# Low parts of three activation operands computed by VectorE alone, and the first two weight tiles behind each multiplied high parts first

## The chip, the cores and the metric

The kernel runs on one core of a Trainium2 chip. The metric is the device time of one execution in microseconds (us), lower is better. TensorE does the matrix products, VectorE (DVE in the rows) and ScalarE (ACT) the elementwise work, GpSimd (POOL) some of it, and SyncE (SP) issues the transfers between HBM and SBUF.

## What is computed

The reference runs two transformer-like blocks in fp32 on one sequence of 1024 tokens with 1024 features, one after the other. Cut to what matters here:

```python
def first_block(x, ...):
    x = x + _hgrn2_mixer(_rmsnorm(x, norm_mix), w_in, ..., w_out)
    x = x + _squared_relu_mlp(_rmsnorm(x, norm_mlp), mlp_w1, mlp_w2)   # a = relu(h @ w1); (a * a) @ w2
    return _rmsnorm(x, norm_final)

def gated_merge(h, y_four, y_attn, w_gate, w_fo, w_ao, w_o):
    g_f, g_a = split(sigmoid(h @ w_gate))
    merged = g_f * (y_four @ w_fo) + g_a * (y_attn @ w_ao)
    return merged @ w_o

def second_block(x, ...):
    hx = modulate(rms_norm(x, norm1_g), sh1, sc1)
    ...                                             # Fourier mixing, neighbourhood attention
    x = x + g1 * gated_merge(hx, y_four, y_attn, ...)
    hx2 = modulate(rms_norm(x, norm2_g), sh2, sc2)
    x = x + g2 * sqrelu_mlp(hx2, w_mlp1, w_mlp2)
    return x
```

Both MLPs have 4096 hidden features.

## The kernel before

Activations lie feature-major in SBUF: 8 slices (index k) of 128 features by 1024 tokens. A product with a 1024x1024 weight is made in 8 output tiles (index m) of 128 features, each held in one of four PSUM buffers of 128x1024 and accumulated over the 8 slices k. To keep fp32 accuracy with the faster fp32r format, every operand is split in two: a high part (the value rounded to fp32r) and a low part (the value less its high part). A product is then three: high weight by high activation, low weight by high activation, high weight by low activation. A 128x512 matmul is issued for each half of the tokens, so one tile of 8 slices takes 32 matmuls with high activations (L415 and L418) and 16 with low ones (L431, or L425 in a tile that is finished by halves).

The class `Operand` names an activation operand: its high part, its low part, the slices that are made in halves, and `lo_on`, which says for each slice whether DVE ("v") or POOL ("p") subtracts. `on_dve` gives all eight to DVE, `even_pool` and `odd_pool` give every second slice to POOL. Three operands matter here:

- HM is the normalised input of the first MLP, HN that of the second. `normed` (L1573, DVE) multiplies each slice by gain and 1/rms into `HT`; `norm_hi` (L1123, or L1125 with a shift, ACT) rounds it into `Hh`; `norm_lo` subtracts into `Hl` (L1583 or L1585 on DVE, L2035 on POOL). `HT` and `Hl` are the same memory. For HN the shift of the modulation is added too: ACT does it in the rounding, DVE in the subtraction, and for the slices of POOL a further ACT instruction adds it to `HT` first (L1129).
- HG is the merged, gated value. In front of it stands the merging loop over m: ACT makes the two sigmoids (L1526), DVE multiplies the Fourier branch by its gate (L1987), multiplies tile m of the attention output product ("ao", weights w_ao) by the other (L1991), and adds (L1993). Then ACT rounds (L1529) and DVE and POOL subtract (L1996, L2096). The attention output's own operand, `yah` and `yal`, lies in the memory of `Hh`, so the rounding into `Hh` can start only when the last "ao" tile is complete.

Weights come in the order of the list `WT`. SP loads weight n into `Wraw` (2 buffers), ACT makes `Whi` (L1094), DVE makes `Wlo` (L1555), both in rings of 4 buffers. `feed(to)` does this up to a weight number; `upto(name)` allows for four weights ahead of the named one. Weight n needs the buffer of weight n-4, and so waits in the engine's queue until the last product with weight n-4 is complete. Each engine runs its own program in the order in which it is written, and they meet at semaphores.

On TensorE, `fm(name, operand)` makes one output tile: for each k the matmuls with high activations, then all with low ones:

```python
for k in range(kt):
    ...  # wait for high part of slice k: 2 matmuls with wh, 2 with wl
for k in range(kt):
    pe.wait_ge(opd.lo_at(k))
    for c in HALF:
        i = e.matmul(t[:, c], wh[:, k, ms], opd.lo[:, k, c], start=False, stop=k == kt - 1)
```

`sums` makes the sums over features for a norm, with a matrix of ones (L491, L494), `square` the squares for it, `rstd` the 1/rms (L1114, L1116). `mlp(j, operand)` makes 32 tiles "s1" of the hidden layer and, mixed with them, the second product "s2" (L649, L651, L658). "wo2" is the product with w_o behind HG. `x_load` brings back the residual into `R1` once a merged slice has been split.

Of the kernel before, what the change touches and what calls it, by code (L numbers as in the profile page):

```python
# [6 lines left out]
F = mybir.dt.float32  # L7
# [84 lines left out]
def build(nc, xT, vecs, w_in, w_out, m_w1, m_w2, ctxT, c_d, w_ada, w_in2, gains, biasE, biasM, w_gate, w_fo, w_ao,  # L92
          w_o2, m2_w1, m2_w2, ident_d, masks_d, rope_d, dft_d, cd_d, out):
    with ExitStack() as ctx:
# [241 lines left out]
        HM = Operand(3, Hh, Hl, (0,), even_pool)  # L336
        HC = Operand(4, hch, hcl, (), even_pool)
        H2 = Operand(5, Hh, Hl, (0,), on_dve)
        HG = Operand(6, Hh, Hl, (), odd_pool)
        HN = Operand(7, Hh, Hl, (0,), even_pool)  # L340
# [33 lines left out]
        def tensor_program(pe):  # L374
# [29 lines left out]
            def fm(name, opd, kt=8, w=None, m0=0, halves=False, ring="all"):  # L404
# [23 lines left out]
# [4 lines that stand above are left out]
                    if k == kt - 1:  # L432
                        full(i, b, occ)
                    if k % 2:
                        yield

# [189 lines left out]
            def mlp(j, opd):  # L626
                A_h, A_l = ah[j], al[j]
                for kind, i in MLP:
                    if kind == "s1":
                        run(fm((j, "s1", i), opd))  # L630
                        continue
# [275 lines left out]
            for m in range(8):  # L907
# [171 lines left out]
        def scalar_program(act):  # L1079
# [442 lines left out]
            for m in range(8):  # L1522
                feed(upto(("w_ao", m - m % 2)))
                for buf, name in ((gfb, "gf"), (gab, "ga")):
                    act.wait_ge(S("merge_in", m % 4).at(m))
                    e.activation(buf[m % 4][:], buf[m % 4][:], ACT.Sigmoid).then_inc(*S(name).tick(m))  # L1526
            for k in range(8):
                act.wait_ge(S("merged").at(k), full_at(("ao", 7)))
                e.activation(Hh[:, k, :], R1[:, k, :], ACT.Copy).then_inc(*S("hi", 6).tick((k, 0)))  # L1529
# [5 lines left out]
            norm_hi(HN, HT, mc(24))  # L1535
# [8 lines left out]
        def vector_program(dve):  # L1544
# [438 lines left out]
            for m in range(8):  # L1983
                feed(upto(("w_ao", m - m % 2)))
                name, o = ("ao", m), mr2[m % 2]
                dve.wait_ge(S("gf").at(m), S("merge_in", m % 4).at(m))
                e.tensor_tensor(R1[:, m, :], R1[:, m, :], gfb[m % 4][:], ALU.mult).then_inc(*S("fo_gate").tick(m))  # L1987
                dve.wait_ge(S("ga").at(m), full_at(name), S("o_full").at((1, NP - 1)))
# [5 lines left out]
            for k in range(0, 8, 2):  # L1994
                dve.wait_ge(HG.hi_at(k), S("merged").at(k), full_at(("ao", 7)))
                e.tensor_tensor(Hl[:, k, :], R1[:, k, :], Hh[:, k, :].bitcast(F), ALU.subtract).then_inc(  # L1996
# [20 lines left out]
        def gpsimd_program(pool):  # L2017
# [53 lines left out]
            norm_lo(HM, HT)  # L2071
# [22 lines left out]
            for k in range(1, 8, 2):  # L2094
                pool.wait_ge(HG.hi_at(k), S("merged").at(k), full_at(("ao", 7)))
                e.tensor_tensor(Hl[:, k, :], R1[:, k, :], Hh[:, k, :].bitcast(F), ALU.subtract).then_inc(  # L2096
                    *S("lo", 6, "p").tick(k))
            norm_lo(HN, HT, True)

# [113 lines left out]
```

## Time and profile before

| | |
|---|---|
| time, median of 3 runs | 2884.84 us (2884.38 to 2887.16) |
| time of the profiled execution | 2886.22 us |
| its span | 2884.4 us |
| TensorE busy | 2780.8 us (96%) |
| VectorE busy | 1318.2 us (46%) |
| ScalarE busy | 894.0 us (31%) |
| GpSimd busy | 215.9 us (7%) |

The span runs from the first to the last instruction of the profiled execution. A matmul on TensorE counts as busy from its start to its end, and neighbours overlap, so the granted clock has to be read beside the share: TensorE runs at 1.2 or at 2.4 GHz, and 1.00 in the rows is the upper level.

### The profile page before, as it was taken

To read this page: it belongs to the slowest core of one execution; us is meant where nothing else is said; L and a number is where in the kernel's file an instruction comes from. 1 tells how busy PE (TensorE), PEld (TensorE's weight loads), DVE (VectorE), ACT (ScalarE), POOL (GpSimd) and SP (SyncE) were. 2 spreads that over 40 slices of the span, in tenths; PEclk is the share of its full clock that TensorE was granted. 3 is DMA by queue.
4 is the path that set the end of the run, shared out by engine and by line. 5 is a ranking of instruction groups with operands and counts; after the bars stand their busy time and mean duration, and the time that the engine had idled before them with its cause. 6 is when DMAs were issued, how large, how long until landed. Compare 5 with 4: busy or idle time off the path is not lost.

```text
span 2884.4 us, 40780 instructions
## 1 busy us (share of the span) xinstructions
PE 2780.8 (96%) x17644; PEld 2316.4 (80%) x17644; DVE 1318.2 (46%) x1637; ACT 894.0 (31%) x1308; POOL 215.9 (7%) x165
## 2 busy tenths in 40 slices
PE   7999999989999999998899999999898999999999
PEld 5887887768888888887789778877786888888887
DVE  5444464455444454336524565565635333333332
ACT  5444454432211112125322443344324111221111
POOL 1222122110000000005200000000101000000000
PEclk9999999999999999999899999999999999999999
DMA  3101110313334442112323221111721111111111
GB/s 127 38 27 42 38 38 24 102 52 116 123 103 132 131 127 70 52 60 78 111 85 110 65 77 50 52 66 47 259 59 37 52 44 52 46 49 51 44 51 66
DMA packets 211266, 213.08 MB, mean 74 GB/s; under 512 B 6928, under 2 KB 186640, under 8 KB 211088
## 3 DMA queue, kind: packets, MB, share of 16 engines
q1 hardware_dynamic: 211088, 210.48, 23.0%
q8 instruction: 139, 2.28, 0.3%
q14 instruction: 39, 0.32, 0.0%
HBM read 188.44 MB, written 22.02 MB: 73 GB/s over the span
## 4 chain that ended last, share of the span: by engine, by line
PE 74%; DVE 4%; ACT 3%; issue 1%; POOL 1%; DMA 0%; ACTq 0%; DVEq 0%; POOLq 0%; SPq 0%
PE ps L415 11%; PE ps L431 11%; PE ps L418 11%; PE ps L658 8%; PE ps L651 7%; PE ps L649 7%; PE ps L844 2%; PE ps L845 2%; PE ps L849 2%; PE ps L478 2%; PE ps L474 2%; PE ps L476 2%; DVE HT L1573 1%; PE ps L819 1%; PE ps L798 1%
## 5 line engine op out<-in xcount | busy, mean ns | idle before, releaser
L1555 DVE TENSOR_TENSOR Wlo<-Wraw,Whi 128x1024 fp32r<-128x1024 f32 x216 | 268.0, 1245 | 991.1 <-ACT Whi L1094 991.1
L1094 ACT ACTIVATE Whi<-Wraw 128x1024 fp32r<-128x1024 f32 x228 | 239.7, 1057 | 1295.6 <-PE ps L431 627.6
L415 PE MATMUL ps<-Hh,Whi 128*128 128x512 f32 x1600 | 505.8, 398 | 30.2 <-DVE k L1627 10.3
L418 PE MATMUL ps<-Hh,Wlo 128*128 128x512 f32 x1600 | 500.5, 394 | 0.0
L649 PE MATMUL ps<-ah,Whi 128*128 128x512 f32 x1024 | 398.8, 389 | 1.2 <-ACT ah L1271 1.2
L651 PE MATMUL ps<-ah,Wlo 128*128 128x512 f32 x1024 | 398.4, 389 | 0.0
L431 PE MATMUL ps<-Hl,Whi 128*128 128x512 f32 x1568 | 384.0, 394 | 2.9 <-DVE Hl L1996 2.7
L415 PEld LDWEIGHTS ps<-Hh,Whi 128*128 128x128 f32 x1600 | 301.9, 191 | 100.5 <-issue 13.0
L418 PEld LDWEIGHTS ps<-Hh,Wlo 128*128 128x128 f32 x1600 | 305.2, 191 | 65.0
L431 PEld LDWEIGHTS ps<-Hl,Whi 128*128 128x128 f32 x1568 | 293.3, 189 | 68.7 <-DVE Hl L1996 3.5
L658 PE MATMUL ps<-al,Whi 128*128 128x512 f32 x1024 | 253.4, 389 | 0.1
L474 PE MATMUL ps<-Whi,Hh 128*128 128x256 f32 x768 | 223.9, 292 | 10.5 <-ACT Hh L1125 10.5
L649 PEld LDWEIGHTS ps<-ah,Whi 128*128 128x128 f32 x1024 | 192.2, 188 | 42.0 <-ACT ah L1271 2.1
L478 PE MATMUL ps<-Whi,Hl 128*128 128x256 f32 x768 | 220.5, 287 | 5.4 <-DVE Hl L1585 5.4
L658 PEld LDWEIGHTS ps<-al,Whi 128*128 128x128 f32 x1024 | 192.0, 188 | 40.8 <-DVE al L1741 1.0
L651 PEld LDWEIGHTS ps<-ah,Wlo 128*128 128x128 f32 x1024 | 192.2, 188 | 39.9
L476 PE MATMUL ps<-Wlo,Hh 128*128 128x256 f32 x768 | 219.3, 285 | 0.0
L474 PEld LDWEIGHTS ps<-Whi,Hh 128*128 128x128 f32 x768 | 149.3, 194 | 12.5 <-issue 11.0
L478 PEld LDWEIGHTS ps<-Whi,Hl 128*128 128x128 f32 x768 | 148.9, 194 | 7.7 <-DVE Hl L1585 7.7
L476 PEld LDWEIGHTS ps<-Wlo,Hh 128*128 128x128 f32 x768 | 149.4, 194 | 0.0
L1594 DVE SCALAR_TENSOR_TENSOR R<-ps,mods,R 128x1024 f32<-128x1024 f32 (+1 forms) x73 | 92.3, 1266 | 69.3 <-PE ps L658 69.3
L844 PE MATMUL ps<-Hh,Whi 128*128 128x512 f32 x256 | 106.8, 417 | 1.6 <-ACT Vx L1481 1.6
(292 smaller groups left out, 3414.1 us busy)
## 6 DMA issues: line engine op xcount, KB each, us to landing
Wraw<-in_m_w SPq DMA_DIRECT2D x128, 512.0 KB, 3.9
n<-in_w_ada SPq DMA_DIRECT2D x64, 512.0 KB, 3.5
Wraw<-in_w_in SPq DMA_DIRECT2D x56, 512.0 KB, 4.0
R<-in_xT SPq DMA_DIRECT2D x16, 512.0 KB, 4.5
Wraw<-in_w_gate SPq DMA_DIRECT2D x16, 512.0 KB, 4.1
gate_scratch<-gr SPq DMA_DIRECT2D x32, 256.0 KB, 2.3
Wraw<-in_w_out SPq DMA_DIRECT2D x8, 512.0 KB, 4.5
xs_scratch<-R SPq DMA_DIRECT2D x8, 512.0 KB, 3.2
```

Source lines behind the costliest of these rows:

```text
L415: e.matmul(t[:, c], wh[:, k, ms], opd.hi[:, k, c], start=k == 0, stop=False)
L418: e.matmul(t[:, c], wl[:, k, ms], opd.hi[:, k, c], start=False, stop=False)
L431: i = e.matmul(t[:, c], wh[:, k, ms], opd.lo[:, k, c], start=False, stop=k == kt - 1)
L474: e.matmul(o, opd.hi[:, k, c], wh[:, k % 4, :], start=k == 0, stop=False)
L476: e.matmul(o, opd.hi[:, k, c], wl[:, k % 4, :], start=False, stop=False)
L478: i = e.matmul(o, opd.lo[:, k, c], wh[:, k % 4, :], start=False, stop=k == 7)
L649: e.matmul(ps[:, cs], wh[:, k, ws], A_h[:, t % 5, cs], start=k == 0, stop=False)
L651: e.matmul(ps[:, cs], wl[:, k, ws], A_h[:, t % 5, cs], start=False, stop=False)
L658: x = e.matmul(ps[:, cs], wh[:, k, ws], A_l[:, t % 5, cs], start=False, stop=k == 3)
L844: e.matmul(t, wh[:, k, :], Hh[:, k, c], start=k == 0, stop=False)
L1094: e.activation(Whi[n % 4][:], Wraw[n % 2][:], ACT.Copy).then_inc(*S("w_hi").tick(n))
L1555: e.tensor_tensor(Wlo[n % 4][:], Wraw[n % 2][:], Whi[n % 4][:].bitcast(F), ALU.subtract).then_inc(*S("w_lo", "v").tick(n))
```

## The change

For HM and HN the low parts of all eight slices are now DVE's (`on_dve`), for HG too; POOL has no part in any of them, and the additional ACT instruction for HN falls away. A new function `two_tiles` makes the first two "s1" tiles of each MLP and the first two "wo2" tiles: all matmuls with high activations of both tiles, then all with low ones. HG's high part goes to the memory of `Hl`, which is free while the "ao" tiles are made, and its low part to that of `Hh`; so the rounding waits for the merged slice (and for the last gate product, which read `Hl`), and only the subtraction waits for the last "ao" tile. In the merging loop `feed` stands behind the sigmoids of an odd m on ACT, and behind the gating of the Fourier branch of an even m on DVE, where it stood at the head of each even m.

```diff
-        HM = Operand(3, Hh, Hl, (0,), even_pool)
+        HM = Operand(3, Hh, Hl, (0,), on_dve)
...
-        HG = Operand(6, Hh, Hl, (), odd_pool)
-        HN = Operand(7, Hh, Hl, (0,), even_pool)
+        HG = Operand(6, Hl, Hh, (), on_dve)
+        HN = Operand(7, Hh, Hl, (0,), on_dve)
...
+            def two_tiles(names, opd):
+
+                both = []
+                for name in names:
+                    both.append((weight(name), take(name)))
+                    WL[WN[name]] = PS[name][0], (PS[name][1], 0)
+                for (n, wh, wl), (b, occ) in both:
+                    empty(b, occ)
+                    pe.wait_ge(S("w_hi").at(n))
+                    for k in range(8):
+                        for hf, c in enumerate(HALF):
+                            pe.wait_ge(opd.hi_at(k, hf))
+                            e.matmul(psum[b][:, c], wh[:, k, :], opd.hi[:, k, c], start=k == 0, stop=False)
+                        pe.wait_ge(lo_of(n))
+                        for c in HALF:
+                            e.matmul(psum[b][:, c], wl[:, k, :], opd.hi[:, k, c], start=False, stop=False)
+                for (n, wh, wl), (b, occ) in both:
+                    for k in range(8):
+                        pe.wait_ge(opd.lo_at(k))
+                        for c in HALF:
+                            i = e.matmul(psum[b][:, c], wh[:, k, :], opd.lo[:, k, c], start=False, stop=k == 7)
+                    full(i, b, occ)
...
                     if kind == "s1":
-                        run(fm((j, "s1", i), opd))
+                        if i == 0:
+                            two_tiles([(j, "s1", 0), (j, "s1", 1)], opd)
+                        elif i > 1:
+                            run(fm((j, "s1", i), opd))
...
-            for m in range(8):
+            two_tiles([("wo2", 0), ("wo2", 1)], HG)
+            for m in range(2, 8):
                 run(fm(("wo2", m), HG, halves=m == 7))
...
             for m in range(8):
-                feed(upto(("w_ao", m - m % 2)))
                 for buf, name in ((gfb, "gf"), (gab, "ga")):
                     act.wait_ge(S("merge_in", m % 4).at(m))
                     e.activation(buf[m % 4][:], buf[m % 4][:], ACT.Sigmoid).then_inc(*S(name).tick(m))
+                if m % 2:
+                    feed(upto(("w_ao", m - 1)))
             for k in range(8):
-                act.wait_ge(S("merged").at(k), full_at(("ao", 7)))
-                e.activation(Hh[:, k, :], R1[:, k, :], ACT.Copy).then_inc(*S("hi", 6).tick((k, 0)))
+                act.wait_ge(S("merged").at(k))
+                if k == 0:
+                    act.wait_ge(S("g_full").at((1, NP - 1)))
+                e.activation(HG.hi[:, k, :], R1[:, k, :], ACT.Copy).then_inc(*S("hi", 6).tick((k, 0)))
...
-            norm_hi(HN, HT, mc(24))
+            norm_hi(HN, HT, mc(24), on_vector=True)
...
             for m in range(8):
-                feed(upto(("w_ao", m - m % 2)))
                 name, o = ("ao", m), mr2[m % 2]
                 dve.wait_ge(S("gf").at(m), S("merge_in", m % 4).at(m))
                 e.tensor_tensor(R1[:, m, :], R1[:, m, :], gfb[m % 4][:], ALU.mult).then_inc(*S("fo_gate").tick(m))
+                if m % 2 == 0 and m:
+                    feed(upto(("w_ao", m - 2)))
...
-            for k in range(0, 8, 2):
+            feed(upto(("w_ao", 6)))
+            for k in range(8):
                 dve.wait_ge(HG.hi_at(k), S("merged").at(k), full_at(("ao", 7)))
-                e.tensor_tensor(Hl[:, k, :], R1[:, k, :], Hh[:, k, :].bitcast(F), ALU.subtract).then_inc(
+                e.tensor_tensor(HG.lo[:, k, :], R1[:, k, :], HG.hi[:, k, :].bitcast(F), ALU.subtract).then_inc(
                     *S("lo", 6, "v").tick(k))
...
-            norm_lo(HM, HT)
...
-            for k in range(1, 8, 2):
-                pool.wait_ge(HG.hi_at(k), S("merged").at(k), full_at(("ao", 7)))
-                e.tensor_tensor(Hl[:, k, :], R1[:, k, :], Hh[:, k, :].bitcast(F), ALU.subtract).then_inc(
-                    *S("lo", 6, "p").tick(k))
-            norm_lo(HN, HT, True)
```

The order on TensorE at the start of the first MLP, before; Whi_55 and Wlo_59 are the weights of tile "s1" 0, Whi_56 and Wlo_60 those of tile 1:

```order
L415 MATMUL ps<-Hh,Whi_55 128x512 x2
L418 MATMUL ps<-Hh,Wlo_59 128x512 x2
L431 MATMUL ps<-Hl,Whi_55 128x512 x16
L415 MATMUL ps<-Hh,Whi_56 128x512 x2
L418 MATMUL ps<-Hh,Wlo_60 128x512 x2
```

The same place in the changed program, at the seam between the two tiles and at the end of them:

```order
L449 MATMUL ps<-Hh,Whi_55 128x512 x2
L452 MATMUL ps<-Hh,Wlo_59 128x512 x2
L449 MATMUL ps<-Hh,Whi_56 128x512 x2
L452 MATMUL ps<-Hh,Wlo_60 128x512 x2
...
L457 MATMUL ps<-Hl,Whi_55 128x512 x16
L457 MATMUL ps<-Hl,Whi_56 128x512 x16
L415 MATMUL ps<-Hh,Whi_57 128x512 x2
```

The 16 matmuls with `Hl` of tile 0 have moved behind the 32 high ones of tile 1. The third tile (Whi_57) follows as it did.

The order on ScalarE at the end of the merging loop and behind it, before; the gf and ga are the sigmoids of m = 4 to 7, Whi_57 and Whi_58 are high parts of "wo2" weights:

```order
L1094 ACTIVATE Whi_57<-Wraw_53 128x1024
L1526 ACTIVATE gf_174<-gf_174 128x1024
L1526 ACTIVATE ga_178<-ga_178 128x1024
L1526 ACTIVATE gf_175<-gf_175 128x1024
L1526 ACTIVATE ga_179<-ga_179 128x1024
L1094 ACTIVATE Whi_58<-Wraw_54 128x1024
L1526 ACTIVATE gf_176<-gf_176 128x1024
L1526 ACTIVATE ga_180<-ga_180 128x1024
L1526 ACTIVATE gf_177<-gf_177 128x1024
L1526 ACTIVATE ga_181<-ga_181 128x1024
L1529 ACTIVATE Hh<-R_49 128x1024 x8
```

The same place in the changed program:

```order
L1552 ACTIVATE gf_175<-gf_175 128x1024
L1552 ACTIVATE ga_179<-ga_179 128x1024
L1121 ACTIVATE Whi_57<-Wraw_53 128x1024
L1552 ACTIVATE gf_176<-gf_176 128x1024
L1552 ACTIVATE ga_180<-ga_180 128x1024
L1552 ACTIVATE gf_177<-gf_177 128x1024
L1552 ACTIVATE ga_181<-ga_181 128x1024
L1121 ACTIVATE Whi_58<-Wraw_54 128x1024
L1559 ACTIVATE Hl<-R_49 128x1024 x8
```

The four last sigmoids now stand ahead of Whi_58, the high part that has to wait for the last "ao" tile; only that one instruction is left between this wait and the eight roundings.

On VectorE at the same place, the changed program has these rows from the merging of m = 7 on:

```order
L2022 TENSOR_TENSOR mr_183<-ga_181,ps 128x1024
L2024 TENSOR_TENSOR R_49<-R_49,mr_183 128x1024
L1585 TENSOR_TENSOR Wlo_62<-Wraw_54,Whi_58 128x1024
L2028 TENSOR_TENSOR Hh<-R_49,Hl 128x1024 x8
```

The low part Wlo_62 stood ahead of the gating of m = 6, and the subtractions are eight here, where they were four with four more on POOL.

## Rows read from the trace of the kernel before

**Rows 1.** The page, busy time of each engine.

```profile
PE 2780.8 (96%) x17644; PEld 2316.4 (80%) x17644; DVE 1318.2 (46%) x1637; ACT 894.0 (31%) x1308; POOL 215.9 (7%) x165
```

**Rows 2.** Busy time by stretch: PE, PEld, DVE, ACT, POOL, TensorE clock, DMA, GB/s.

```profile
615.00:651.00 36.00, 28.70 (x100) 20.39 (x101) 27.77 (x17) 15.85 (x18) 12.79 (x4) 0.86 0.22 74
700.00:750.00 50.00, 50.00 (x222) 41.41 (x221) 22.64 (x27) 7.75 (x8) 0.00 (x0) 1.00 0.41 135
2061.00:2097.00 36.00, 27.28 (x102) 21.29 (x101) 22.70 (x13) 14.81 (x16) 12.40 (x4) 0.86 0.45 147
2167.00:2204.00 37.00, 30.74 (x101) 21.49 (x100) 26.73 (x16) 19.13 (x21) 11.73 (x4) 0.82 0.06 19
```

**Rows 3.** Waits of TensorE: us in total, times, longest us.

```profile
PE ps L415 <- ACT Hh L1123: 7.6, 6, 2.4
```

**Rows 4.** Timeline of DVE and POOL, start of the first MLP: start, us, instruction.

```profile
618.38 4.59 DVE L1573 SCALAR_TENSOR_TENSOR HT<-R,vec,t 128x1024 f32<-128x1024 f32 x2
621.70 2.47 DVE L1573 SCALAR_TENSOR_TENSOR HT<-R,vec,t 128x1024 f32<-128x1024 f32 x2
627.43 3.37 DVE L1573 SCALAR_TENSOR_TENSOR HT<-R,vec,t 128x1024 f32<-128x1024 f32 x1
631.92 6.80 DVE L1583 TENSOR_TENSOR Hl<-HT,Hh 128x1024 fp32r<-128x1024 f32 x4
618.08 2.61 POOL L2035 TENSOR_TENSOR Hl<-HT,Hh 128x1024 fp32r<-128x1024 f32 x1 [77.00 <-ACT Hh L1123]
```

**Rows 5.** Timeline of ACT and PE, the same place.

```profile
630.84 2.26 ACT L1123 ACTIVATE Hh<-HT 128x1024 fp32r<-128x1024 f32 x2 [2.24 <-DVE HT L1573]
617.99 0.59 PE L415 MATMUL ps<-Hh,Whi 128*128 128x512 f32 x1 [0.37 <-ACT Hh L1123]
622.92 0.73 PE L415 MATMUL ps<-Hh,Whi 128*128 128x512 f32 x2 [1.24 <-ACT Hh L1123]
628.65 1.22 PE L415 MATMUL ps<-Hh,Whi 128*128 128x512 f32 x2 [2.14 <-ACT Hh L1123]
```

**Rows 6.** Timeline of DVE: an operand with all subtractions on DVE, POOL idle.

```profile
1377.79 9.64 DVE L1585 SCALAR_TENSOR_TENSOR Hl<-HT,mods,Hh 128x1024 fp32r<-128x1024 f32 x8
```

**Rows 7.** Chain that ended last, pieces of three stretches: start, us, what.

```profile
650.45 0.45 PE ps L415 x2
...
2061.87 1.06 ACT Whi L1094
...
2096.84 0.45 PE ps L415 x2
...
2104.09 3.63 PE ps L431 x16
...
2187.55 0.85 PE ps L418 x2
...
2203.76 0.45 PE ps L415 x2
```

**Rows 8.** Timeline, end of the merging loop and the first "wo2" tiles.

```profile
2066.62 7.67 ACT L1529 ACTIVATE Hh<-R 128x1024 fp32r<-128x1024 f32 x8
2067.81 1.19 PE L415 MATMUL ps<-Hh,Whi 128*128 128x512 f32 x2 [6.03 <-ACT Hh L1529]
2072.21 0.69 PE L418 MATMUL ps<-Hh,Wlo 128*128 128x512 f32 x2
2072.11 11.20 DVE L1996 TENSOR_TENSOR Hl<-R,Hh 128x1024 fp32r<-128x1024 f32 x4
2093.41 1.06 ACT L1094 ACTIVATE Whi<-Wraw 128x1024 fp32r<-128x1024 f32 x1 [17.81 <-DMA Wraw<-in_w_o]
```

**Rows 9.** Timeline, start of the second MLP.

```profile
2169.68 13.36 DVE L1573 SCALAR_TENSOR_TENSOR HT<-R,modA,b 128x512 f32<-128x512 f32 x8 [0.41 <-ACT b L1116]
2179.49 1.15 ACT L1125 ACTIVATE Hh<-HT,mods 128x1024 fp32r<-128x1024 f32 x1 [2.17 <-DVE HT L1573]
2171.25 0.76 PE L415 MATMUL ps<-Hh,Whi 128*128 128x512 f32 x1 [0.37 <-ACT Hh L1125]
2177.38 1.07 PE L415 MATMUL ps<-Hh,Whi 128*128 128x512 f32 x2
```

## The prediction

> **What bounds the kernel now.** I read the page's busy times first: TensorE is busy for 96% of the span and no other engine for half of it [rows 1]. So only two things can shorten the run: TensorE's idle time, 103.6 us in all, and stretches in which its matmuls run at the lower clock. A table of busy time by stretch shows where these lie. Inside an MLP TensorE is busy for 50.00 of 50.00 us at clock 1.00. At the three places that the change touches it is busy for 28.70 of 36, 27.28 of 36 and 30.74 of 37 us, at 0.82 to 0.86 [rows 2]. I call them A (the first MLP's start), B (merging and "wo2") and C (the second MLP's start). The list of waits says what TensorE waits for there: high parts from ScalarE [rows 3]. The timelines then say who is late behind ScalarE.
>
> At A it is DVE. `normed` instructions follow each other after 1.2 us where nothing is in the way (two in 2.47 us), but one that starts while POOL subtracts takes 3.37 us, and the one at 618.38 ends, by the start of its follower, after 3.4 us [rows 4]. The subtractions come behind them, from 631.92. The last high part is therefore ready at 630.84 + 2.26 = 633.1, TensorE waits up to 2.14 us on the way [rows 5], and the third tile starts at 650.45 [rows 7]. At C it is the same with a 13.36 us row of `normed` [rows 9], and the third tile starts at 2203.76 [rows 7].
>
> At B the last "ao" tile is complete at 2061.87, when ACT converts a weight; then come four sigmoids, and the rounding starts at 2066.62 [rows 7, 8]. TensorE idles for 6.03 us. The low parts of DVE are late too: the four end at 2072.11 + 11.20 = 2083.3 [rows 8].
>
> **The change part by part.** Matmuls cost 3.63 us per 16 at the upper clock [rows 7], so 0.227 us each: 0.91 for one slice's four high ones, 7.26 for a tile's 32, 3.63 for its 16 low ones. At the lower level a pair takes 0.85 [rows 7], a slice 1.7.
>
> *A.* Eight subtractions and eight `normed` all run on DVE without POOL. For the subtraction with nothing on POOL there is a row from elsewhere: eight in 9.64 us, 1.2 each [rows 6]. `normed` of k = 2 starts at 618.38 as before; six slices at 1.195 end at 625.6; ACT adds 1.06 (two take 2.26): high part 7 at 626.7. The subtractions end at 625.6 + 9.6 = 635.2. TensorE starts on k = 0 as before, its second half at 617.99, at the lower clock. It was at the upper one by 622.92 [rows 5]. Until then it falls behind the 1.2 us pace of the slices (1.7 each), and catches up at 0.91. Slice 7 is then done at 627.6 (bound by the high part) to 628.1 (if the clock rises as late as 624.5); I take 627.8. Behind it stand 32 high matmuls of tile 1, to 635.1, and 32 low ones, to 642.3. The low parts are all there at 635.2, the first one is wanted at 635.1 and the last 3.2 us after it: they cost nothing, with 3 us to spare. Gain 650.45 - 642.3 = **8.1 us**.
>
> *C.* `normed` of k = 1 follows 0.66 us after 2169.68, seven slices at 1.195 end at 2178.7. ACT needs 1.15 for one, so the last high part is at 2179.9. ACT has lost four instructions of 1.15 us, which only shortens its queue. The lower clock lasted from 2171.25 to the mixed row at 2177.38 [rows 9], longer than at A. So slices 0 to 3 end at 2172.7, 2174.5, 2176.2, 2177.9, and the other four at about 0.93: 2181.6. Then 14.5 us: 2196.1, where the chain has 2203.76 [rows 7]. Subtractions end at 2178.7 + 9.6 = 2188.3, before the first is wanted (2188.9). Gain **7.6 us**, 8.6 if the clock is no brake.
>
> *B.* ACT's weight conversion at 2061.87 still waits for the last "ao" tile; it ends at 2062.9, and the eight roundings follow directly at 0.95 us each (eight in 7.67, the last taking 1.04 [rows 8]): high part 0 at 2063.9, 7 at 2070.6. This holds if the merged slices are there. Slice 7 needs the last tile (2061.87), two DVE instructions of 1.15 to 1.25: 2064.3, ahead of its turn at 2069.6. Its sigmoids wait only for their transfer, which SP issues when slice 3 is merged. TensorE's idle time falls from 6.03 to about 2.0 us. After 1.24 us of idleness at A the next matmuls were at the upper clock, after 2.14 us at the lower [rows 5]. 2.0 is nearest to the second, so I take the lower clock for 4.6 us, as long as here before (2067.81 to the mixed row at 2072.21 [rows 8]). Slices end at 2065.9, 2067.6, 2069.0, then five at 0.91: 2073.5. With 14.5 us more: 2088.0 against 2096.84 [rows 7]. Gain **8.8 us**; 10.7 if the clock stays up, 7.9 if it is down for 6.5 us. The low parts: DVE makes Wlo_62 until 2065.5, then eight subtractions to 2075.1, wanted from 2080.8. What may be late next is the fifth "wo2" weight, whose transfer stands behind the eight residual loads and was converted at 2093.41 [rows 8]. Each load waits for a low part, and the last low part falls from 2083.3 to 2075.1, so these too come 8 us earlier; the weight is wanted two tiles after tile 1, at 2109.8. Nothing is lost.
>
> *Moved feeds and queues.* In the merging loop conversions of "wo2" weights wait for "ao" tiles 1, 3, 5, 7 as before; only what is behind them changes. On SP nothing is moved, but it waits for low parts of weights from DVE that come one gating (1.2 us) later. The weights are wanted 10 us and more after that. In `two_tiles` tile 0 of A ends at 638.7, and its weight buffer is free then; the next to use it is tile "s1" 4, wanted at 642.3 + 21.8 = 664.1. POOL does nothing at these places any more, and nobody waits for it.
>
> *The sum.* 8.1 + 8.8 + 7.6 = 24.5 us. After each place TensorE runs without a gap (50.00 of 50.00 [rows 2]), so a gain is handed on to the end. The profiled execution took 2886.22, so 2861.7; it was 1.4 us over the median, so the median comes to **2860.3**.
>
> **Where a rule speaks against it.** The four DVE instructions that I add at each place are 4 x 1.2 = 4.8 us on an engine that was already full there (27.77 of 36 us [rows 2], and without a gap from 616.5 to 638.7). The Trainium skill, page "Perfetto Trace Analysis", section "Optimizing Scalar/DVE Operations", holds that with DVE saturated it may make sense to move work to ScalarE or even GpSimd, which is what the kernel before did; though it adds that between DVE and GpSimd this might not help, because they share a port. By its first half alone taking the work back would be a loss of DVE time and the sum that of the second rival below, 2871; by its second half 2860. The trace's 3.37 us beside POOL against 1.2 without it [rows 4, 6] agrees with the second.
>
> **The rivals.**
> *DVE's 3.4 us are not POOL's doing*, but come from ACT or TensorE reading the same tiles, and the subtractions suffer likewise. Then `normed` at A ends at 631.9 as before, eight subtractions of 3.4 us end at 659.1, and the second tile at 659.1 + 0.45 + 3.63 = 663.2: 12.7 us later. At C 2183.0 + 27.2 + 4.1 = 2214.3, 10.5 later; at B nothing. Time 2884.8 + 23 = 2908, slower. It decides from 1.8 us a subtraction on (631.9 + 8 x 1.8 + 4.1 = 650.4 at A). For it: the 3.4 us rows lie where ACT and TensorE are busy too. Against it: eight in 9.64 us, while TensorE multiplies the same operand [rows 6]. Chance 0.02.
>
> *The slow `normed` stay slow, the subtractions take 1.2.* At A high part 7 comes at 633.1 as before; its slice at the lower clock ends at 634.8, both tiles at 649.3, gain 1.1. The low parts, at 631.9 + 9.6 = 641.5, are in time. At C `normed` ends at 2169.68 + 13.36 = 2183.0, the high part at 2184.2, its slice at 2185.9, the tiles at 2200.4, gain 3.4. With B's 8.8: 2871.5. For it: a busy ACT or TensorE is beside every slow one. Against it: POOL's subtraction runs from 618.08 to 620.7, and the instruction behind it ends one undisturbed length later. Chance 0.05. This is what the first half of the rule above (the Trainium skill, "Perfetto Trace Analysis") would come to.
>
> *The clock stays down for the whole first tile*, since TensorE is fed in small pieces. Eight slices at 1.7 us from 617.7: 631.3, gain 4.6 at A; 2172.7 + 7 x 1.7 = 2184.6, gain 4.6 at C; 2065.9 + 7 x 1.7 = 2077.8, gain 4.5 at B; sum 13.7, time 2871. For it: at 2187.55, at the end of a run of unbroken slices, pairs still took 0.85 [rows 7]. Against it: fed in smaller pieces, it still rose at 622.92, 2072.21 and 2177.38. Chance 0.08.
>
> *The merged slices, not ScalarE, set B's pace*, because transfers of the gates come late. They run behind SP's waits and keep the DMA queues full in that stage. Each us by which the last sigmoid comes after 2061 moves B's end by one; the whole of the 4 us gained in idleness would be gone with transfers 4 us late, and then the gain is 4.8: 2864.3. Chance 0.07.
>
> **How the numbers follow.** My case has 0.78. With every brake released (8.6 + 10.7 + 8.3 = 27.6) it gives 2857.2, with the long low clock at B and 1 us less at A and C 2863.2. The range goes down to 2857.0 and up to 2867.0, so that it holds the late gates too and leaves the two other clocks and the port out. A measurement here tells 0.2% (5.8 us) from no change. All cases but the first rival are beyond it: faster 0.96, same 0.02, slower 0.02.
>
> **What the profile after would show.** No POOL row at the three places; `normed` and subtractions in unbroken rows of about 8.9 and 9.6 us; at B a wait of TensorE near 2 us in place of 6.03; the rounding starting 1.1 us after the last "ao" tile; no wait for a low part. The prediction is wrong if `normed` still has instructions of 3.4 us, if TensorE waits for the eighth subtraction, or if 0.85 us pairs run through all of the first tile.

## The result, and the profile after

The changed kernel takes 2857.37 us (median of 4 runs, 2857.24 to 2858.25), the kernel before 2884.95 us (4 runs, 2884.38 to 2887.16). The ratio is 0.9904, with a 95% interval of 0.9889 to 0.992: faster by 27.6 us. The forecast was 2860.3 us in a range of 2857.0 to 2867.0. The profiled execution took 2857.45 us.

The page after, its busy times (before: [rows 1]):

```profile
span 2855.6 us, 40766 instructions
PE 2766.6 (97%) x17644; PEld 2308.2 (81%) x17644; DVE 1307.7 (46%) x1649; ACT 890.7 (31%) x1304; POOL 176.9 (6%) x153
```

TensorE issues the same 17644 matmuls. It is busy for 14.2 us less, so about that much of the gain is matmuls that no longer run at the lower clock; the rest of the 28.8 us between the spans is idle time.

The table by stretch, at the three places (PE, PEld, DVE, ACT, POOL, TensorE clock, DMA, GB/s; before: [rows 2]):

```profile
615.00:651.00 36.00, 35.02 (x142) 27.19 (x143) 27.26 (x24) 16.80 (x17) 0.00 (x0) 0.95 0.26 88
2052.00:2089.00 37.00, 36.93 (x156) 30.35 (x157) 17.89 (x17) 13.03 (x13) 0.00 (x0) 0.95 0.52 171
2150.00:2187.00 37.00, 36.93 (x149) 29.42 (x150) 24.99 (x21) 15.47 (x15) 0.00 (x0) 0.92 0.09 29
```

TensorE now runs through each of them almost without a gap, and the mean clock, which was 0.82 to 0.86 before, is 0.92 to 0.95. POOL has nothing there.

Timeline of DVE and ACT at A (before: [rows 4, 5]):

```profile
614.97 9.12 DVE L1603 SCALAR_TENSOR_TENSOR HT<-R,vec,t 128x512 f32<-128x512 f32 x8 [0.42 <-ACT t L1143]
624.01 9.16 DVE L1613 TENSOR_TENSOR Hl<-HT,Hh 128x1024 fp32r<-128x1024 f32 x8
616.95 8.24 ACT L1150 ACTIVATE Hh<-HT 128x1024 fp32r<-128x1024 f32 x7 [0.56 <-DVE HT L1603]
```

Neither the eight `normed` nor the eight subtractions hold a slow instruction. The last high part is there at 616.95 + 8.24 = 625.19.

Timeline of TensorE at A:

```profile
611.18 1.98 PE L517 MATMUL ps<-kST,ones 128*128 128x512 f32 x4 [2.01 <-ACT kST L1133]
615.60 0.47 PE L449 MATMUL ps<-Hh,Whi 128*128 128x512 f32 x1 [2.43 <-ACT Hh L1150]
...
619.08 0.99 PE L452 MATMUL ps<-Hh,Wlo 128*128 128x512 f32 x2
...
626.27 0.62 PE L449 MATMUL ps<-Hh,Whi 128*128 128x512 f32 x2
...
633.53 7.42 PE L457 MATMUL ps<-Hl,Whi 128*128 128x512 f32 x32
640.78 0.61 PE L415 MATMUL ps<-Hh,Whi 128*128 128x512 f32 x2
```

Pairs of 0.99 us stop at 619.9: from there the clock is up. The second tile's high products start at 626.27, directly behind the first's. The 32 low ones of both tiles stand in one unbroken row, and the third tile starts at 640.78.

The end of the merging loop and the first "wo2" tiles (before: [rows 7, 8]):

```profile
2046.76 1.04 ACT L1552 ACTIVATE ga<-ga 128x1024 f32<-128x1024 f32 x1
2049.92 1.06 ACT L1121 ACTIVATE Whi<-Wraw 128x1024 fp32r<-128x1024 f32 x1 [2.12 <-PE ps L431]
2050.88 7.68 ACT L1559 ACTIVATE Hl<-R 128x1024 fp32r<-128x1024 f32 x8
...
2047.85 1.98 PE L431 MATMUL ps<-yal,Whi 128*128 128x512 f32 x8
2052.07 0.70 PE L449 MATMUL ps<-Hl,Whi 128*128 128x512 f32 x2 [2.25 <-ACT Hl L1559]
...
2053.59 1.05 PE L452 MATMUL ps<-Hl,Wlo 128*128 128x512 f32 x2
...
2056.15 0.96 PE L449 MATMUL ps<-Hl,Whi 128*128 128x512 f32 x2
...
2068.31 7.42 PE L457 MATMUL ps<-Hh,Whi 128*128 128x512 f32 x32
2075.56 0.61 PE L415 MATMUL ps<-Hl,Whi 128*128 128x512 f32 x2
...
2053.45 9.16 DVE L2028 TENSOR_TENSOR Hh<-R,Hl 128x1024 fp32r<-128x1024 f32 x8
```

TensorE's wait is 2.25 us where it was 6.03 [rows 8]. The last sigmoid ends at 2047.8, and ACT is then idle for 2.12 us in front of a weight conversion that waits for the last "ao" tile. (Hl and Hh have changed roles here: Hl holds the high parts.) TensorE starts at the upper clock; only from 2053.6 to 2056.9 do pairs take 1.05 us.

The start of the second MLP (before: [rows 9]):

```profile
2144.79 3.01 PE L517 MATMUL ps<-b,ones 128*128 128x512 f32 x4 [2.07 <-ACT b L1133]
2149.94 1.63 PE L449 MATMUL ps<-Hh,Whi 128*128 128x512 f32 x2 [2.14 <-ACT Hh L1152]
...
2155.13 0.96 PE L452 MATMUL ps<-Hh,Wlo 128*128 128x512 f32 x2
...
2167.87 7.42 PE L457 MATMUL ps<-Hl,Whi 128*128 128x512 f32 x32
2175.13 0.62 PE L415 MATMUL ps<-Hh,Whi 128*128 128x512 f32 x2
...
2158.26 9.65 DVE L1615 SCALAR_TENSOR_TENSOR Hl<-HT,mods,Hh 128x1024 fp32r<-128x1024 f32 x8
```

**Where the time came from.** I cut both timelines at the same instructions: at A and C from the first of the four matmuls that close the sum of squares (L494 before, L517 after; "the closing sum" below) to the start of the third tile, at B from the start of the last "ao" tile's low products to the start of the third "wo2" tile, the point of [rows 7]. In the kernel before the closing sums at A and C are these:

```profile
612.73 1.98 PE L494 MATMUL ps<-kST,ones 128*128 128x512 f32 x4 [2.01 <-ACT kST L1106]
...
2165.90 1.98 PE L494 MATMUL ps<-b,ones 128*128 128x512 f32 x4 [2.07 <-ACT b L1106]
```

The last column of the table runs from the start of the first MLP's third tile to the first matmul of the "ao" tiles; nothing is edited in it. All in us, the kernels of the experiments below included:

| kernel | A | B | C | third tile to "ao" |
|---|---|---|---|---|
| before | 37.6 | 36.9 | 37.7 | 1366.1 |
| before, again | 37.5 | 36.8 | 37.7 | 1366.4 |
| after | 29.6 | 27.7 | 30.3 | 1363.6 |
| after, again | 29.6 | 27.7 | 30.6 | 1364.3 |
| subtractions on DVE alone | 33.5 | 32.1 | 36.9 | 1363.3 |
| two_tiles alone | 37.1 | 31.9 | 37.1 | 1363.0 |
| merging edits alone | 37.5 | 31.0 | 37.7 | 1365.7 |
| high parts not in free memory | 29.6 | 27.7 | 30.6 | 1363.9 |
| conversion last | 29.6 | 24.2 | 30.8 | 1363.5 |
| slices outside, tiles inside | 28.5 | 27.7 | 29.6 | 1365.0 |
| both of these | 28.4 | 23.6 | 29.9 | 1367.6 |
| POOL multiplies at A | 37.2 | 27.7 | 30.2 | 1363.0 |
| POOL fills at A | 29.6 | 27.7 | 30.5 | 1364.0 |

The gains are 7.95, 9.16 and 7.36 us: 24.5 of the 28.8 us between the two profiled executions. Of the rest, 1.55 lie ahead of A, 2.5 in the last column and 0.3 behind C, where nothing is edited.

The medians show such an excess too, and nearly everywhere. Against the kernel before that was run beside it, every kernel with an edit at A and C is faster by more than its three places give: 27.6 us where they give 24.5, and in the experiments below by 1.6 to 3.9 us more. Even with `two_tiles` alone, where A and C hardly get shorter, it is 8.9 for 6.0. The merging edits alone, which leave A and C as they were, bring 4.9 us by the medians and 5.8 at the places. (The lengths of the places come from one profile each.)

### The profile page after: what moved, and what is told of

Read it like the earlier page. It is cut to its first block, busy times and chain, and to the rows that moved or that the text cites. A ratio compares the mean times of both kernels' runs of the same rounds, so it can differ in the third digit from the quotient of the medians.

```text
span 2855.6 us, 40766 instructions
## 1 busy us (share of the span) xinstructions
PE 2766.6 (97%) x17644; PEld 2308.2 (81%) x17644; DVE 1307.7 (46%) x1649; ACT 890.7 (31%) x1304; POOL 176.9 (6%) x153
## 4 chain that ended last, share of the span: by engine, by line
PE 75%; DVE 3%; ACT 3%; issue 1%; POOL 1%; DMA 0%; ACTq 0%; POOLq 0%; DVEq 0%; SPq 0%
PE ps L415 10%; PE ps L418 10%; PE ps L431 10%; PE ps L684 8%; PE ps L675 8%; PE ps L677 8%; PE ps L870 2%; PE ps L871 2%; PE ps L875 2%; PE ps L501 2%; PE ps L497 2%; PE ps L499 2%; PE ps L845 1%; PE ps L824 1%; ACT Whi L1121 1%
## 5 line engine op out<-in xcount | busy, mean ns | idle before, releaser
L415 PE MATMUL ps<-Hh,Whi 128*128 128x512 f32 x1408 | 438.2, 392 | 10.3 <-DVE k L1657 10.3
L418 PE MATMUL ps<-Hh,Wlo 128*128 128x512 f32 x1408 | 435.9, 391 | 0.0
L431 PE MATMUL ps<-Hl,Whi 128*128 128x512 f32 x1392 | 339.4, 393 | 0.0
L415 PEld LDWEIGHTS ps<-Hh,Whi 128*128 128x128 f32 x1408 | 263.2, 189 | 64.6 <-DVE k L1657 10.8
L418 PEld LDWEIGHTS ps<-Hh,Wlo 128*128 128x128 f32 x1408 | 265.5, 189 | 55.8
L431 PEld LDWEIGHTS ps<-Hl,Whi 128*128 128x128 f32 x1392 | 259.6, 188 | 56.5 <-issue 3.3
L870 PE MATMUL ps<-Hh,Whi 128*128 128x512 f32 x256 | 106.7, 417 | 1.6 <-ACT Vx L1508 1.6
```

What stands on the lines that cost most here:

```text
L415: e.matmul(t[:, c], wh[:, k, ms], opd.hi[:, k, c], start=k == 0, stop=False)
L418: e.matmul(t[:, c], wl[:, k, ms], opd.hi[:, k, c], start=False, stop=False)
L870: e.matmul(t, wh[:, k, :], Hh[:, k, c], start=k == 0, stop=False)
```

## The experiments

**The changed kernel once more**, for what repeats.

> The changed kernel once more, beside its variants on the same chip: 2857.4 us within 1 us. In its profile against the kernel before: A 8.0, B 9.1, C 7.4 us shorter as in the first profile. The stretch between A and B was 2.5 us shorter there, without an edit in it; if that is chance of the transfers, it will differ from 2.5 us here, if it comes from the change, it will be 2.5 us again.

2857.85 us (2857.11 to 2860.6, 4 runs), ratio 0.9907, interval 0.9892 to 0.9922. The three places repeat within 0.3 us. Its start-up does not: the closing sum at A begins at 613.4 instead of 611.2. The stretch without an edit is 1.8 us shorter than before, where the first profile had 2.5.

**All subtractions on DVE, nothing else.**

```
-        HM = Operand(3, Hh, Hl, (0,), even_pool)
+        HM = Operand(3, Hh, Hl, (0,), on_dve)
-        HG = Operand(6, Hh, Hl, (), odd_pool)
-        HN = Operand(7, Hh, Hl, (0,), even_pool)
+        HG = Operand(6, Hh, Hl, (), on_dve)
+        HN = Operand(7, Hh, Hl, (0,), on_dve)
...
-            for k in range(0, 8, 2):
+            for k in range(8):
                 dve.wait_ge(HG.hi_at(k), S("merged").at(k), full_at(("ao", 7)))
...
```

(Not shown: POOL's subtractions and ACT's added shift for HN fall away.)

> The kernel before with one part of the change: the low parts of HM, HN and HG all on VectorE, nothing on GpSimd, no extra shift on ScalarE; no two_tiles, merging as before. Theory (GpSimd's subtractions block VectorE): normed in unbroken 1.2 us instructions; the last high part at A about 6.4 us earlier, but the low parts, now eight in a row on one engine, end the first tile. A gains 4.4 us, C 4.1, B 4.9, time about 2871.6 us (2869 to 2875). Rival (VectorE is slow for another reason and only gets more work): normed keeps instructions of 3.4 us and the time is 2885 to 2908 us.

2871.67 us (2870.28 to 2872.95, 4 runs), ratio 0.9953, interval 0.9938 to 0.9968. A gives 4.0 us, B 4.8, C only 0.8. DVE at A has the same two rows of 9.12 and 9.16 us as the whole change. The timeline of TensorE at C shows what is missing without `two_tiles`, and in its first row a loss that comes before it:

```profile
2153.79 3.64 PE L494 MATMUL ps<-b,ones 128*128 128x512 f32 x4 [2.07 <-ACT b L1106]
...
2172.81 0.72 PE L431 MATMUL ps<-Hl,Whi 128*128 128x512 f32 x2 [0.46 <-DVE Hl L1585]
...
2176.40 0.73 PE L431 MATMUL ps<-Hl,Whi 128*128 128x512 f32 x2 [0.46 <-DVE Hl L1585]
2177.59 1.22 PE L431 MATMUL ps<-Hl,Whi 128*128 128x512 f32 x2 [0.46 <-DVE Hl L1585]
2178.61 1.06 PE L415 MATMUL ps<-Hh,Whi 128*128 128x512 f32 x2
...
2181.12 0.62 PE L418 MATMUL ps<-Hh,Wlo 128*128 128x512 f32 x2
```

Each pair of low products, 0.45 us of work, waits for its subtraction, one every 1.2 us. The sixth such pair, at 2177.59, runs at the lower level, and the clock is down until 2181. The expectation had 4.1 us for C and nothing for this fall. The 3.4 us at the lower level cost, by estimate, half their length, 1.7 us; another 1.3 were lost ahead of it: the closing sum ran at the lower level here (3.64 us, where it takes 1.98 before), and `normed` began its row of eight 5.06 us behind the sum's start instead of 3.78. That the median comes out as expected all the same is luck: the places give 9.6 us, and 3.7 of the 13.3 between the profiled executions lie outside them.

**`two_tiles` alone** (the function and its two calls, as in the change; subtractions shared with POOL, merging as before).

> The kernel before with two_tiles alone at the three places; GpSimd keeps its share. Theory: at A and C the last high part is what is late, so reordering brings 0.4 and 0.9 us; at B the low parts are late by 2.7 us and the reordering hides them, about 4.8 us. Time about 2878.8 us (2876 to 2882). Rival (late low parts are the main loss everywhere and two_tiles the main gain): 2870 us or less.

2876.31 us (2874.49 to 2877.32, 6 runs), ratio 0.9968, interval 0.9956 to 0.9981. B gives 5.0 us, A and C 0.45 and 0.6 (at C the closing sum again took 3.64 us, so that `normed` began 1.3 us later there). At A `normed` is as slow as before (timeline of DVE):

```profile
615.55 15.49 DVE L1600 SCALAR_TENSOR_TENSOR HT<-R,vec,t 128x512 f32<-128x512 f32 x8 [0.42 <-ACT t L1143]
630.96 6.79 DVE L1610 TENSOR_TENSOR Hl<-HT,Hh 128x1024 fp32r<-128x1024 f32 x4
```

The high parts set the pace there, and an order that hides late low parts finds hardly any to hide. The expectation was 2878.8 us; the places came out as expected (6.0 us for 6.1), and the 2.5 us that the median is lower lie outside them.

**The edits of the merging alone** (the moved feeds, HG in exchanged memory, its shorter wait).

```
-        HG = Operand(6, Hh, Hl, (), odd_pool)
+        HG = Operand(6, Hl, Hh, (), odd_pool)
...
             for m in range(8):
-                feed(upto(("w_ao", m - m % 2)))
...
+                if m % 2:
+                    feed(upto(("w_ao", m - 1)))
...
```

> The kernel before with only the merging edits: feeds moved in the merging loop, HG's high part in the memory of Hl and its low part in that of Hh; GpSimd keeps its share, no two_tiles. Theory: TensorE's wait before the first wo2 tile falls from 6.0 to 2.2 us, low parts start earlier but stay slow, about 5 us at B: 2879.9 us (2877 to 2883). A and C unchanged. Rival (DMA sets the merging): wait stays over 4 us and the time is within 2 us of before.

2880.32 us (2878.17 to 2882.55, 10 runs), ratio 0.9984, interval 0.9974 to 0.9993. A and C do not move, B gives 5.8. TensorE's wait is short, but the low parts are now what is late (timelines of DVE and PE):

```profile
2063.88 13.42 DVE L2001 TENSOR_TENSOR Hh<-R,Hl 128x1024 fp32r<-128x1024 f32 x4
...
2062.50 1.19 PE L415 MATMUL ps<-Hl,Whi 128*128 128x512 f32 x2 [2.24 <-ACT Hl L1532]
...
2074.05 1.20 PE L431 MATMUL ps<-Hh,Whi 128*128 128x512 f32 x4 [0.65 <-DVE Hh L2001]
...
2077.36 1.21 PE L431 MATMUL ps<-Hh,Whi 128*128 128x512 f32 x4 [2.11 <-DVE Hh L2001]
```

Four subtractions beside POOL's four take 13.42 us, against 9.16 for all eight on DVE alone.

**The changed kernel without the free memory:** high parts back in Hh, and with them the wait for the last "ao" tile.

```
-        HG = Operand(6, Hl, Hh, (), on_dve)
+        HG = Operand(6, Hh, Hl, (), on_dve)
...
-                act.wait_ge(S("merged").at(k))
-                if k == 0:
-                    act.wait_ge(S("g_full").at((1, NP - 1)))
+                act.wait_ge(S("merged").at(k), full_at(("ao", 7)))
```

> The changed kernel with HG's high part back in the memory of Hh and its low part in Hl, so that the rounding waits for the last ao tile again; the moved feeds stay. Theory: the weight conversion in front of the roundings waits for the same tile anyway, so the memory brings nothing: within 1 us of the changed kernel, 2857.4 us, TensorE's wait before wo2 2.2 to 2.3 us. Rival (the free memory is what shortened the wait): the wait goes back to 4 us or more and the time to 2859.5 to 2862 us.

2857.73 us (2856.58 to 2859.47, 4 runs), ratio 0.9905, interval 0.9891 to 0.992; B is the same to 0.1 us. The free memory does nothing here. The rounding stands behind a conversion that waits for that same tile, so it could not have started earlier anyway. Of the merging edits, then, it is the moved feeds that shorten TensorE's wait (6.03 us with the subtractions or `two_tiles` alone, 2.25 here).

**The last conversion behind the rounding**, on ACT and on DVE (shown for ACT), so that the free memory comes to use.

```
-                if m % 2:
+                if m % 2 and m < 7:
                     feed(upto(("w_ao", m - 1)))
...
                 e.activation(HG.hi[:, k, :], R1[:, k, :], ACT.Copy).then_inc(*S("hi", 6).tick((k, 0)))
+            feed(upto(("w_ao", 6)))
```

> The changed kernel with the last weight conversion of the merging loop behind the eight roundings on ScalarE, and behind the eight subtractions on VectorE. Theory (that conversion, which waits for the last ao tile, is what is left of the wait; the free memory now comes to use): the roundings of the first seven slices are done before the last ao tile ends, TensorE's wait of 2.25 us goes and its clock stays at 2.4 GHz, so the first wo2 tile's high products end 4.0 us earlier: 2853.4 us (2852.5 to 2855). Rival (the later conversion is wanted too early, or transfers behind it come late): a new wait at the fourth wo2 tile, 2857 us or more.

2854.85 us (2854.48 to 2855.93, 4 runs), ratio 0.9896, interval 0.9881 to 0.991: 3.5 us less at B, 2.5 in the medians. Timelines of ACT and PE:

```profile
2046.98 1.06 ACT L1552 ACTIVATE gf<-gf 128x1024 f32<-128x1024 f32 x1 [3.52 <-DMA R<-fo_scratch]
...
2048.89 7.68 ACT L1559 ACTIVATE Hl<-R 128x1024 fp32r<-128x1024 f32 x8
2056.48 1.04 ACT L1121 ACTIVATE Whi<-Wraw 128x1024 fp32r<-128x1024 f32 x1
...
2047.98 1.97 PE L431 MATMUL ps<-yal,Whi 128*128 128x512 f32 x8
2050.08 0.70 PE L449 MATMUL ps<-Hl,Whi 128*128 128x512 f32 x2
```

TensorE has almost no wait left (0.13 us) and keeps the upper clock. What now sets ACT's start is the last sigmoids, which wait for a transfer (3.52 us), and behind them 0.95 us a slice. So the roundings start only 1.06 us ahead of the end of the last "ao" tile (2048.89 against 2049.95), and not seven slices ahead as expected. Those 1.06 us are all that the free memory can have given directly; the conversion moved away is about as long. How the 3.5 us, the clock that no longer falls among them, divide between the two was not run.

**Slices outside, tiles inside.** With the loops exchanged in `two_tiles`, TensorE has both tiles' products (1.8 us) for each slice that comes.

```
...
-                    for k in range(8):
+                for k in range(8):
+                    for (n, wh, wl), (b, occ) in both:
...
```

> The changed kernel with two_tiles walking slice by slice over both tiles in its high products, 8 matmuls a slice (1.82 us) instead of 4 (0.91 us), so that TensorE does not run out of slices at VectorE's pace of 1.2 us. Theory: the 0.2 to 0.3 us waits for each slice at A go, gain 1.1 us there, 0.5 us at C, nothing at B: 2855.8 us (2855 to 2857). Rival (the clock rises later or falls, or the first tile's later end delays what reads it): no change or slower by up to 1 us.

2856.91 us (2855.94 to 2859.65, 4 runs), ratio 0.9904, interval 0.9887 to 0.992. A gives 1.1 us more, C 0.7; in the medians the 0.5 us are within the scatter.

**Both together.**

> Both edits, the late conversion and the walk slice by slice: gains add, 4.0 + 1.6 us, time 2851.8 us (2850.5 to 2854). Rival: at B ScalarE's 0.95 us a slice no longer matters and the walk slice by slice takes the buffers later, gains overlap, 2853.5 us.

2853.15 us (2852.64 to 2853.82, 4 runs), ratio 0.9889, interval 0.9874 to 0.9904: the best version, 4.2 us ahead of the changed kernel by the medians (4.7 ahead of its second run, which was made beside this one). The expected 5.6 us are there at the places (5.7), but the stretch without an edit took 1367.6 us in this profile, 4.0 more than in the first of the changed kernel.

**Is it POOL that slows `normed`?** The whole change moves many things, so I put back only POOL: at A it multiplies two tiles of an earlier stage into a third that nobody reads, as often as it subtracted before, and waits for the same high parts. This adds work and leaves nothing out. A second kernel puts a fill of one tile in the same place, which reads nothing. (In both, ACT and DVE wait for the last of these instructions when they take up the first tile of the hidden layer; not shown.)

```
+            for k in range(0, 8, 2):
+                pool.wait_ge(HM.hi_at(k, 0), HM.hi_at(k))
+                if k:
+                    pool.wait_ge(S("noise").at(k - 2))
+                e.tensor_tensor(Tb[:], acc[:], Pt[:], ALU.mult).then_inc(*S("noise").tick(k))
```

(In the second: `e.memset(Tb[:], 0.0).then_inc(...)`.)

> The changed kernel with four instructions of no use on GpSimd at A: after the high parts of slices 0, 2, 4, 6 it multiplies two other 128x1024 SBUF tiles into a third, where it subtracted before; VectorE and ScalarE wait for them only long after. Theory (GpSimd's two-input instruction and VectorE's exclude each other, whatever tiles they read): normed shows 3.4 us instructions again, the last high part comes about 6 us later, time 2862.5 to 2865.5 us. Rival (it was the sharing of HT and Hh by three engines, or ScalarE and TensorE): no change, 2857.4 us.

> The same with a memset of a 128x1024 tile in place of the multiplication, so that GpSimd writes SBUF but reads none of it. If every GpSimd access shuts VectorE's two-input instructions out, normed is slow as with the multiplication, 2860 us or more; if only a GpSimd instruction that reads SBUF does, as the Trainium skill has it (SBUF - State Buffer), normed stays at 1.2 us and the time at 2857.4 us.

The multiplications: 2865.43 us (2864.58 to 2865.52, 4 runs), ratio 0.9934, interval 0.9919 to 0.9949; A is back at 37.2. (The expectation's upper end was 2865.5.) The fills: 2857.6 us (2856.48 to 2858.53, 4 runs), ratio 0.9906, interval 0.989 to 0.9923; A is 29.6. Timelines of DVE and POOL, first with multiplications:

```profile
616.17 15.47 DVE L1605 SCALAR_TENSOR_TENSOR HT<-R,vec,t 128x512 f32<-128x512 f32 x8 [0.42 <-ACT t L1143]
631.57 11.34 DVE L1615 TENSOR_TENSOR Hl<-HT,Hh 128x1024 fp32r<-128x1024 f32 x8
...
622.60 6.77 POOL L2113 TENSOR_TENSOR Tb<-acc,Pt 128x1024 f32<-128x1024 f32 x2 [2.25 <-ACT Hh L1150]
```

then with fills:

```profile
615.63 9.12 DVE L1605 SCALAR_TENSOR_TENSOR HT<-R,vec,t 128x512 f32<-128x512 f32 x8 [0.42 <-ACT t L1143]
...
617.17 0.95 POOL L2113 MEMSET Tb<- 128x1024 f32 x1 [76.97 <-ACT Hh L1150]
```

The same tiles are read by TensorE and ACT in both, and the tiles that POOL reads are others. So the slowness comes from POOL's multiplication itself and from nothing that ACT or TensorE do. A POOL instruction that reads only one tile was not run. The Trainium skill, page "SBUF — State Buffer", section "Who interferes with whom", states that a DVE instruction with two inputs from SBUF contends with a GpSimd instruction that reads SBUF, and not with one that only writes it. The two runs agree with it: 15.47 us beside reading instructions, 9.12 beside fills.

**The kernel before once more**, for what the stretches without an edit do.

> The kernel before, unchanged, with a second profile. The three places of the edits account for 24.4 us of the difference between the kernels, and the medians differ by 27.6. Theory 1: the rest is chance between profiled executions and between runs: here too the stretch from the third tile of the first MLP to the first "ao" tile takes anything from 1363 to 1367 us (1366.07 in the first profile), the three places read 37.5, 80.3 and 37.7 us again, and the ratio against the kernel before is 1.000 within 0.001. Theory 2: the changed kernel really is 2.5 us shorter in that stretch, where nothing was edited: then it reads 1366 again here, within 0.3 us, and the start-up in front of the first MLP's norm is again 1.5 us longer than in the changed kernel (612.7 against 611.2).

2884.33 us (2881.73 to 2887.3, 11 runs), ratio 0.9998, interval 0.9989 to 1.0007. The stretch between A and "ao" took 1366.4 us again. That is against my first theory, as far as one execution goes; the start-up (start of the closing sum at A), 613.1 here and 611.2 and 613.4 in the changed kernel, is against the second. The tables by stretch show what the 2.5 us are. First the kernel before, again, 50 us and more behind the start of the eight subtractions of [rows 6]:

```profile
1427.98:1437.98 10.00, 6.94 (x58) 6.73 (x57) 0.23 (x1) 2.91 (x3) 2.04 (x1) 0.99 0.19 63
1437.98:1447.98 10.00, 10.00 (x72) 10.00 (x73) 4.79 (x4) 2.11 (x2) 2.73 (x4) 0.84 0.33 107
```

and the same stretches of the changed kernel:

```profile
1418.18:1428.18 10.00, 6.94 (x58) 6.73 (x58) 1.57 (x2) 3.23 (x4) 3.38 (x2) 1.00 0.05 19
1428.18:1438.18 10.00, 10.00 (x86) 10.00 (x85) 3.46 (x3) 1.81 (x2) 1.42 (x3) 1.00 0.32 107
```

The same matmuls with the same gap (6.94 of 10 us busy) ran at 0.84 behind it in the one and at 1.00 in the other: some 1.5 us. Another 0.9 us lie 40 us ahead of it, at clock 0.73 and 0.86. The repeated run of the changed kernel had 0.88 and 0.78 here, and a later stretch of it was 1.8 us shorter in exchange. It is the clock, not the work. Added up over the whole stretch from the traces, TensorE worked at the lower level for 29.0 and 26.7 us in the two profiles of the kernel before and for 19.8 and 20.0 in those of the changed one. What sets it stays open. Pure chance does not fit: the kernels with A as before have 1365.7 to 1366.4, all but one of those with A edited 1363.0 to 1365.0, and the medians have the same excess. Nor is it that A is shorter and everything behind it comes earlier: with `two_tiles` alone and with the multiplications A takes 37 us as before, and the stretch 1363.0. And the kernel with both late edits, at 1367.6, goes the other way.

## Why the prediction was right

**Place A.** The forecast put the last high part at 626.7, the end of tile 0's high products at 627.8 and of both tiles at 642.3. Counted from the closing sum (1.55 us earlier after), it was 625.19 + 1.55 = 626.7, 626.27 + 1.55 = 627.8 and 640.78 + 1.55 = 642.3. The low parts were all there at 634.7, and the first was wanted at 635.1: free, as said. The table gives 7.95 us for the 8.1 forecast.

**Place C.** Forecast 2196.1; in the time of before it is 2165.90 + 30.34 = 2196.2 (the closing sum begins at 2165.90 there). The clock came up 1 us sooner than I had assumed, but the closing sum at 2144.79 already ran low (3.01 us, where 1.98 stand at A and before), and `normed` began 0.65 us later behind it (2149.22 - 2144.79 = 4.43, where it was 2169.68 - 2165.90 = 3.78). The two nearly cancel. 7.4 for 7.6.

**Place B.** The rounding started 1.0 us behind the last "ao" tile (1.1 forecast), TensorE waited 2.25 us (2.0), DVE's eight subtractions took 9.16 (9.6). The clock was mis-sized: I took it as low for 4.6 us from the tile's start; it was low for 3.4, and not at the start. 9.2 us for 8.8. The place was priced rightly, but the merged high parts' free memory, which I let stand as a part of it, was worth nothing; the prediction itself had the conversion wait for the last "ao" tile and did not draw the conclusion.

**The sum.** 24.5 us in the profiled executions, as forecast. The time came out 2.9 us below the forecast: 4.3 us more lie outside the three places, and 1.4 of them are what the profile of before stood over its median. The step that was incomplete is "a gain is handed on to the end": true of the work, but the clock's falls behind later gaps do not come at the same moments again. It covers the 2.5 us shown above in the profiles. That the medians too differ by 3 us more than the three places, and do so in every kernel with A and C edited, is not explained. So it is partly luck that the time fell within the range. It lies 0.4 us above the lower end, and that end stood for a clock that is no brake at B and C, which is not what happened.

**The rivals.** That the 3.4 us were not POOL's doing, or that `normed` stayed slow, is excluded by the 9.12 us rows and by the two kernels with POOL's work put back: with the multiplications A loses 7.6 us and the median is 2865.4. The clock did not stay down for a whole first tile anywhere. The late gates were close: the last sigmoid ended 2.0 us ahead of the last "ao" tile, and when the conversion in front of it was gone, they were what the rounding waited for. DVE's four added subtractions at each place cost nothing together with `two_tiles`, though DVE was full there. The Trainium skill's advice in "Perfetto Trace Analysis", "Optimizing Scalar/DVE Operations", to move work off a saturated DVE holds here only with its own reservation on GpSimd.

**Which part brought what.** Alone, by the medians, the parts bring 13.6, 8.9 and 4.9 us. Their sum, 27.4, is the whole by coincidence, for at the places they do not add up: at A 4.0 + 0.45 + 0 against 7.95 together, at B 4.8 + 5.0 + 5.8 against 9.2. At A and C `two_tiles` has something to hide only when the subtractions have become eight in a row behind `normed`; then A falls from 33.5 to 29.6 us (the merging edits do not touch A). At C it falls from 36.9 to 30.3, a part of which is the clock losses told above. At B all three remove parts of the same delay.

## What to carry to other kernels

A two-operand operation on GpSimd is no free help while DVE reads two operands too and is on the critical path: here three of the four fell beside `normed` and cost DVE 15.47 - 9.12 = 6.35 us there, and all four together saved it four subtractions, 4.8. When operands are split into a high and a low part and the low one comes later, put the high products of several tiles first: here the low ones then cost TensorE no wait. But this pays only once the low parts are what is late (0.45 us at A alone, 3.9 behind the faster `normed`). Before memory is freed to let an operation start earlier, look at what stands in front of it in its engine's queue: one conversion waiting for the same tile made the freed memory worthless, and moving it gave 3.5 us at its place.

## What the runs showed of the hardware

- TensorE's lower clock did not always start with the work behind an idle time: after 2.25 us of idleness at B the first three pairs were at the upper level (0.70 us from 2052.07) and pairs of 1.05 us followed from 2053.6 to 2056.9. At A, after 2.43 us, the first matmul (615.60) still had the upper level, and from 616.44 on, behind another 0.37 us, it was low.
- The clock also fell without a long gap: at C of the kernel with the subtractions alone, pairs that came every 1.2 us with 0.46 us of waiting before each were followed by 3.4 us at the lower level (2177.6 to 2181.0).
- The closing sum at C, four matmuls behind an idle time of 2.07 or 2.08 us, took 1.98 us in both profiles of the kernel before and 3.01 and 3.29 in those of the changed one, 3.64 with the subtractions alone.
- The same gap of 3.06 us was followed by 10 us at 1.00, 0.84 or 0.78 in different executions: by estimate up to 10 x 0.22 = 2.2 us, with no difference in the work.
- Reading instructions of POOL lengthened DVE's eight `normed` from 9.12 to 15.47 us; fills of 0.95 us lengthened nothing.
